# A decoder step in split-precision matmuls: the residual x goes to HBM for the feed-forward stage

## The reference, cut to what matters

```
up = rmsnorm(x, norm_ffn_w) @ w_up            # 1024 -> 2 * 2816
c  = causal_dwconv(up, prefix, conv_w, conv_b)  # width 3, per channel
g, u = c[..., :2816], c[..., 2816:]
x  = x + (silu(g) * u) @ w_down               # 2816 -> 1024
y  = rmsnorm(x, norm_final_w)
```

## Time and profile before

| | |
|---|---|
| median of three runs | 868.1 us |
| span of the profiled execution | 866.2 us |
| what lies around the span (difference to the median) | 1.9 us |
| TensorE busy | 849.0 us (98%) |
| VectorE busy | 553.8 us (64%) |
| ScalarE busy | 364.3 us (42%) |
| GpSimd busy | 76.9 us (9%) |
| granted TensorE clock, mean | 0.996 |

### The profile page before, as it was taken

One profiled execution on the slowest core, in us unless ns is written; L12 is line 12 of the kernel. 1 busy time (PEld: TensorE's weight loads), 2 busy tenths in 40 slices (PEclk: granted clock), 3 DMA queues, 4 the chain that ended last, 5 costly groups with the idle time before them and its releaser, 6 DMA issues.

```text
span 866.2 us, 17354 instructions
## 1 busy us (share of the span) xinstructions
PE 849.0 (98%) x6884; PEld 799.4 (92%) x6884; DVE 553.8 (64%) x981; ACT 364.3 (42%) x652; POOL 76.9 (9%) x149
## 2 busy tenths in 40 slices
PE   6999999999999999999999999999999999999995
PEld 6988878789999999877899999999999999999995
DVE  6444246678574643455355899678697796786754
ACT  6402133366453721344343756244353352443452
POOL 2320000000000000000000321012011110110200
PEclk9999999999999999999999999999999999999998
DMA  9798689721233565579133322223322322231323
GB/s 308 255 369 291 215 325 337 246 93 40 66 99 105 159 248 172 192 270 369 68 110 126 99 65 83 86 77 107 98 86 86 122 75 86 84 102 73 88 78 104
DMA packets 50146, 131.25 MB, mean 152 GB/s; under 512 B 5939, under 2 KB 8503, under 8 KB 49810
## 3 DMA queue, kind: packets, MB, share of 16 engines
q1 hardware_dynamic: 48064, 124.40, 43.5%
q0 software_dynamic: 1712, 5.62, 1.8%
q10 hardware_dynamic: 290, 0.12, 0.1%
HBM read 123.12 MB, written 7.00 MB: 150 GB/s over the span
## 4 chain that ended last, share of the span: by engine, by line
PE 83%; DVE 1%; ACT 0%; issue 0%; DVEq 0%
PE proj L1181 53%; PE proj L1137 3%; PE proj L1198 2%; PE score L1265 2%; PE score L1263 2%; PE score L1264 2%; PE proj L1200 2%; PE proj L1199 2%; PE score L1432 2%; PE T L1265 1%; PE T L1263 1%; PE T L1264 1%; PE score L1398 1%; PE T L1274 1%; PE T L1417 1%; PE score L1467 1%
## 5 line engine op out<-in xcount | busy, mean ns | idle before, releaser
L1181 PE MATMUL proj<-a_hi,w_hi 128*128 128x272 f32 (+1 forms) x740 | 159.7, 290 | 6.4 <-DVE w_lo L1891 6.2
L1532 ACT ACTIVATE w_hi<-w_raw 128x1024 fp32r<-128x1024 f32 (+2 forms) x128 | 118.4, 931 | 109.1 <-PE proj L1181 93.2
L1181 PE MATMUL proj<-a_lo,w_hi 128*128 128x272 f32 (+1 forms) x740 | 158.2, 288 | 0.0
L1181 PE MATMUL proj<-a_hi,w_lo 128*128 128x272 f32 (+1 forms) x740 | 158.0, 288 | 0.0
L1868 DVE TENSOR_TENSOR w_lo<-w_raw,w_hi 128x1024 fp32r<-128x1024 f32 (+2 forms) x128 | 136.3, 1070 | 29.0 <-ACT w_hi L1532 28.8
L1181 PEld LDWEIGHTS proj<-a_hi,w_hi 128*128 128x128 f32 x740 | 118.4, 189 | 13.1 <-issue 6.7
L1181 PEld LDWEIGHTS proj<-a_lo,w_hi 128*128 128x128 f32 x740 | 118.8, 189 | 0.0
L1181 PEld LDWEIGHTS proj<-a_hi,w_lo 128*128 128x128 f32 x740 | 118.4, 189 | 0.0
L1181 PE MATMUL proj<-d_hi,w_hi 128*128 128x272 f32 x448 | 92.5, 287 | 0.0
L1181 PE MATMUL proj<-d_lo,w_hi 128*128 128x272 f32 x448 | 92.1, 287 | 0.0
L1181 PE MATMUL proj<-d_hi,w_lo 128*128 128x272 f32 x448 | 92.1, 288 | 0.0
(11 more groups left out here) (360 smaller groups left out, 1655.7 us busy)
## 6 DMA issues: line engine op xcount, KB each, us to landing
w_raw<-in_w_up SPq DMA_DIRECT2D x28, 512.0 KB, 3.6
w_raw<-in_w_in SPq DMA_DIRECT2D x21, 512.0 KB, 3.8
early_pages<-in_cache_k SPq DMA_DIRECT2D x32, 256.0 KB, 5.8
pages<-in_cache_v SPq DMA_DIRECT2D x32, 256.0 KB, 5.3
c_pages<-in_cache_mem_k SPq DMA_DIRECT2D x16, 512.0 KB, 7.0
c_pages<-in_cache_mem_v SPq DMA_DIRECT2D x16, 512.0 KB, 6.3
p_raw<-in_w_up SPq DMA_DIRECT2D x16, 512.0 KB, 3.9
w_raw<-in_w_down SPq DMA_DIRECT2D x32, 256.0 KB, 2.6
```

What stands on the lines that cost most here:

```text
L1181: mm = pe.matmul(tile_banks(n)[:, half, 0:width], wt, act[:, at, half * HALF:half * HALF + width], start=(k == 0 and a == 0), stop=(k == w ...
L1532: act.activation(w_hi[:, n % W_HI_RING, 0:kt, :], w_raw[:, n % W_RING, 0:kt, :], ACT.Copy).then_inc(w_hi_ready, 1)
```

## The change: what it does

- **x in HBM.** In column 1 SyncE stores x to a new tensor `scratch_x` (step `x_store`, 2.2 MB). The bytes of x in SBUF then hold `p_raw`, `t_raw` and a buffer `down_out`; a second `down_out` lies in `norm_area`. `p_lo` and `t_lo` keep their old places, now apart from the raw data. In column 20, step `x_back` loads x again, in two halves.
- **The 32 adds of columns 4 to 19** are no longer a VectorE addition. ScalarE copies the tile from PSUM to one of the two `down_out` buffers, and GpSimd issues a DMA of it (128 x 544 fp32, 272 KB) that accumulates on `scratch_x`. ScalarE waits before each copy for the accumulating DMA of two tiles earlier. The eight adds of the last group stay on VectorE and wait for the two loads of x.
- **The list of steps of the feed-forward stage is written anew.** TensorE's order of tiles and products is the same. The first pair's weights are loaded in column 4 behind the gate tile's step (before: at the stage's start), since x must be free. Column 4 now makes all three splits of the first pair ahead of its `gate` step. In the later columns, splits, sums and loads of the next pair stand in the paired column, and the last steps of a paired column (`up_in` of the up half, `taps`, `gate`, `act`) stand behind the following gate tile.
- Semaphores are merged: `mix_prefix_loaded` and `fvec_loaded` become one, `rows_loaded` joins `lams_loaded`.

The diff, cut to what the prediction speaks of:

```diff
+    def pair_ends(prev, q):
+        p = PAIRED.index(prev)
+        nearer = [("pair_split", q, 1)], [("pair_hi", q, 2), ("pair_split", q, 2), ("pair_load", q + 1, 1)]
+        ahead, behind = nearer if q < len(PAIRED) else ([], [])
+        return [("pair_out", p, 4)] + ahead + [("up_in", prev, 1)] + behind
+    for i in range(FT):
+        downs = [TILE[step] for step in beside_of(i)]
+        prev_paired = i - 1 in PAIRED
+        if i in PAIRED:
+            q = PAIRED.index(i)
+            more = q + 1 < len(PAIRED)
+            s += [("prod", q, 1), ("prod", q, 2)]
...
+            (hi0, lo0), (hi1, lo1) = (split_next(f) for f in downs)
+            s += [("pair_out", q, 1), ("pair_out", q, 2), ("tile", downs[0])] + hi0
...
+            s += [("prod", q, 5), ("prod", q, 6), ("pair_out", q, 5), ("add", downs[0]), ("pair_out", q, 6)]
+            s += [("sums", q + 1)] * more + [("act", i - 1)] * prev_paired
+            s += [("tile", downs[1])] + hi1 + lo1 + [("pair_hi", q + 1, 0)] * more
+            s += [("prod", q, 7), ("pair_out", q, 7), ("add", downs[1])] + [("pair_split", q + 1, 0)] * more
+            s += [("prod", q, 3)] + [("pair_hi", q + 1, 1)] * more + [("pair_out", q, 3), ("up_in", i, 0), ("prod", q, 4)]
+            s += [("pair_load", q + 2, 0)] * more
             continue
...
+        if prev_paired:
+            s += pair_ends(i - 1, PAIRED.index(i - 1) + 1) + hi0
+            s += [("taps", i - 1, 0)] + lo0 + [("taps", i - 1, 1), ("gate", i - 1), ("up_in", i, 0)] + hi1
+            s += [("act", i - 1)] + lo1 + [("taps", i, 0), ("tile", up_tile), ("up_in", i, 1), ("taps", i, 1), ("gate", i)]
+        elif i + 1 == PAIRED[0]:
+            s += hi0 + hi1 + [("up_in", i, 0)] + lo0 + lo1 + [("pair_load", 0, 0), ("pair_load", 0, 1), ("blend_lo", i - 1), ("taps", i, 0)]
+            s += [("sums", 0), ("tile", up_tile), ("pair_hi", 0, 0), ("pair_hi", 0, 1), ("up_in", i, 1), ("pair_split", 0, 0), ("pair_load", 1, 0)]
+            s += [("pair_hi", 0, 2), ("pair_split", 0, 1), ("taps", i, 1), ("pair_split", 0, 2), ("pair_load", 1, 1), ("gate", i)]
...
+            if i == 1:
+                s.append(("x_store",))
...
+        if i == FT - 2:
+            s.append(("x_back",))
+        for f in downs:
+            hi, lo = split_next(f)
+            s += [("tile", f)] + hi + lo + [("add", f)]
+        s.append(("act", i))
...
+        p_raw = lend(x_area, 0, (2, KT, P))
+        t_raw = lend(x_area, 2 * KT * P, (3, 4, P))
+        down_out = [lend(x_area, 2 * KT * P + 12 * P, (TOK,)), lend(norm_area, 24 * P, (TOK,))]
...
+        def wait_x_free(eng):
+
+            eng.wait_ge(ready["up"], KT)
+            eng.wait_ge(sem("xw_ready"), 8)
+            eng.wait_ge(sem("x_stored"), 16)
...
+                if kind == "x_store":
+                    for n in (KT - 2, KT - 1):
+                        wait_tile_out(sp, TILE["co", "add", n])
+                    sp.dma_start(t["scratch_x"], x[:, :, :]).then_inc(sem("x_stored"), 16)
+                if kind == "x_back":
+                    wait_pair_lo(sp, len(PAIRED) - 1, 2)
+                    for n in range(2):
+                        sp.wait_ge(sem(f"x_added{n}"), 16 * len(X_ADDS[n::2]))
+                    for n in range(2):
+                        sp.dma_start(x[:, 4 * n:4 * n + 4, :], t["scratch_x"][:, 4 * n:4 * n + 4, :]).then_inc(sem(f"x_loaded{n}"), 16)
...
+                if kind == "add" and arg in X_ADDS:
+                    m = X_ADDS.index(arg)
+                    wait_tile_out(pool, arg)
+                    pool.dma_start(t["scratch_x"][:, TILES[arg]["i"], :], down_out[m % 2], accum_op=ALU.add
+                                   ).then_inc(sem(f"x_added{m % 2}"), 16)
...
+                elif kind == "add" and arg in X_ADDS:
+                    m = X_ADDS.index(arg)
+                    act.wait_ge(tile_done, arg + 1)
+                    if m >= 2:
+                        act.wait_ge(sem(f"x_added{m % 2}"), 16 * (m // 2))
+                    else:
+                        wait_x_free(act)
+                    act.activation(halves(down_out[m % 2]), proj[arg % 2][:, :, 0:HALF], ACT.Copy).then_inc(tile_out[arg % 2], 1)
...
-                elif kind == "add":
+                elif kind == "add" and arg not in X_ADDS:
+                    dve.wait_ge(sem(f"x_loaded{TILES[arg]['i'] // 4}"), 32)
```

More of the change, by code:

```diff
@@ L348, in split_next @@
         return [("w_hi", n + 2)] if n + 2 < len(TILES) else [], [("w_lo", n + 2)] if n + 2 < len(TILES) else []
[L350 to L368, removed]
-            continue
[L370 to L390, removed]
-            s.append(("norm", "up"))
[L392 to L404, removed]
@@ new lines, in pair_ends @@
+    def pair_ends(prev, q):
[11 more added lines that the diff above has]
+            if prev_paired:
+                s += pair_ends(i - 1, q)
+            (hi0, lo0), (hi1, lo1) = (split_next(f) for f in downs)
+            s += [("pair_out", q, 1), ("pair_out", q, 2), ("tile", downs[0])] + hi0
+            if prev_paired:
+                s += [("taps", i - 1, 0)] + lo0 + [("taps", i - 1, 1), ("gate", i - 1)]
+            else:
+                s += lo0
+            s += [("prod", q, 5), ("prod", q, 6), ("pair_out", q, 5), ("add", downs[0]), ("pair_out", q, 6)]
[4 more added lines that the diff above has]
+            s += [("pair_load", q + 2, 0)] * more
+            continue
+        gate_tile, up_tile = TILE["up", "gate", i], TILE["up", "up", i]
+        (hi0, lo0), (hi1, lo1) = split_next(gate_tile), split_next(up_tile)
+        s.append(("tile", gate_tile))
+        if i == 0:
+            s.append(("norm", "up"))
+        if prev_paired:
+            s += pair_ends(i - 1, PAIRED.index(i - 1) + 1) + hi0
[5 more added lines that the diff above has]
+            s += [("pair_hi", 0, 2), ("pair_split", 0, 1), ("taps", i, 1), ("pair_split", 0, 2), ("pair_load", 1, 1), ("gate", i)]
+        else:
+            s += hi0 + [("up_in", i, 0)] + lo0
+            if i:
+                s += [("blend_lo", i - 1)] * (i <= 4)
+            if i == 1:
+                s.append(("x_store",))
+            s += [("taps", i, 0), ("tile", up_tile)] + hi1 + [("up_in", i, 1)] + lo1 + [("taps", i, 1), ("gate", i)]
@@ L424 @@
 SCHEDULE = make_schedule()
+X_ADDS = [step[1] for step in SCHEDULE if step[0] == "add" and TILES[step[1]]["phase"] != LAST_DOWN]
 HALVED = {step[1] for step in SCHEDULE if step[0] == "half_tile"}
@@ L982, in _ @@
                 if kind == "pair_load" and arg < len(PAIRED):
[L983 to L987, removed]
+                    j = step[2]
+                    if arg:
+                        wait_pair_lo(sp, arg - 1, j)
+                    else:
+                        wait_x_free(sp)
+                    sp.dma_start(p_raw[:, j, :, :], t["w_up"][((D_FF, 0)[j] + PAIRED[arg] * P) // P, :, :, :]
+                                 ).then_inc(sem(f"slot_landed1_{j}"), 16)
+                if kind == "x_store":
[8 more added lines that the diff above has]
+                        sp.dma_start(x[:, 4 * n:4 * n + 4, :], t["scratch_x"][:, 4 * n:4 * n + 4, :]).then_inc(sem(f"x_loaded{n}"), 16)
                 if kind == "scale":
@@ L2076, in _ @@
                     q, part = step[1:]
[L2077 to L2078 removed]
+                    dve.wait_ge(sem("pair_hi"), 3 * q + part + 1)
+                    if part:
+                        dve.wait_ge(sem("sums_made"), q + 1)
                     if part == 2:
```

33 lines of the change are left out of this document (13 added, 20 removed).

## The result

The changed kernel takes 869.7 us (median of 8 runs, 868.48 to 870.95); the kernel before took 867.44 in the same comparison (8 runs, 866.84 to 869.03). The ratio is 1.0025, 95% interval 1.0015 to 1.0035: slower by about 2.2 us. The profiled execution took 868.48 us with a span of 866.7; it is the fastest of the eight.

The account below looks back on a forecast made before the run. TensorE, busy 849.0 of 866.2 us, was taken to bound the kernel. All terms were 0 except one stop in columns 4 and 5, 0.85 + 0.6 = 1.4 us, added to 868.1: 869.5 us, range 867.4 to 873.0.

Parts of the forecast that it names:

- Adds off VectorE: Columns 4 to 19: 32 adds, 23.0 us, leave VectorE; gain 0, at most 0.24 us, as TensorE waits for nothing.
- Accumulating DMAs: GpSimd's DMAs of down tiles onto x: landing taken as 8 us, bounds 5.5 and 13.8; cost 0.
- the 9.4 us given beside it: Landing of an accumulating DMA estimated from the Trainium skill's figure for GpSimd waiting on the port shared with VectorE.
- the limits of 10.6 and 13.0: Landing times in us above which TensorE's product 7 would wait: 10.6 in the first pair, 13.0 in a steady pair.
- Store and load of x: Store in column 1 (7 us) and reload before the last adds (some 9 us, 20 available): cost 0.
- (a): Column 4: the first pair's load goes out late, so VectorE's sums start 0.5 to 1.5 us late, or 0; 0.6 taken.
- L: Delay of the start of VectorE's sums of the first pair in column 4; 0.6 us taken, range 0 to 1.5.
- (b): Three splits ahead of column 4's gate delay w_lo, so TensorE stops at column 5's first down tile: 0.85 us, bounds 0 to 1.5.
- Sum: Columns 4 and 5: 0.85 + 0.6 = 1.4 us, rounded down; span 867.6, median 869.5 us.
- The stop at the second down tile grows by L: Column 4: TensorE's existing stop of about 0.25 us lengthens by the sums' delay, counted within the 1.4 us.
- Later columns: Even columns behind a pair: VectorE carries 16.7 of 18 us, TensorE's cover is 2.2 us; cost 0.
- Rival D: Faster: VectorE's relief closes hidden TensorE stops, giving at most 867.6 us; head and tail untouched; chance 0.03.

Follow-up runs that it names:

- both edits: Changed kernel with the first pair's load one tile earlier on SyncE and two of its splits back behind the gate: 868.12 us, ratio 1.0007.

## Why the prediction held, and what it missed

- *Adds off VectorE, 0.* Right: 18.7 us less busy time, and no wait of TensorE from 553 to 794.9 us. ScalarE's copy took 0.60 us, under the bound of 0.8.
- *Accumulating DMAs, 0, landing 8.* The cost is right. 7.5 and 7.8 us is what the first pair's two take, while two loads of the next pair and the weights run beside them; the median of all is 4.8. So the value taken was too high for the rest, as was the 9.4 us given beside it, and both stood under the limits of 10.6 and 13.0. ScalarE never waits for one in the changed kernel.
- *Store and load of x, 0.* Right: store 9.3 us, load 6.5 from 807 on, the first add that needs it at 827.08.
- *(a) the late load, L = 0.6.* Right in kind. It was 0.36 in the first profile, 0.15 in the second, and 0.74 to 0.94 in those of the edited kernels that keep it late. The bounds of 0 to 1.5 held all of them; a single value isn't to be had from the rows of before.
- *(b) the splits ahead of the gate, 0.85.* Right in kind, and too small: 1.07 us in every profile of this order in which nothing else waits. The walk along the queues was exact. w_lo ended at 540.7 in before's times, 540.4 without L, which is where the steps put it, and the taps start behind ScalarE's `t_hi`, as worked out. What was off is TensorE's side. The 539.62 of the earlier trace rows is where the chain's previous piece ends; TensorE's own row starts at 539.46, 0.16 earlier. And after a stop the next two matmuls take 0.11 us more.
- *Sum, 1.4.* The stretch grew by 1.43, in part by luck: L came out 0.24 under the value taken and (b) 0.22 over it. That the two simply add is shown: 269.84 + L + 1.07 gives the stretch of six profiles to 0.01 us. "The stop at the second down tile grows by L" held too: `up_in` 0.4.
- *Later columns, 0.* Right: with both edits the stretch is before's to 0.01 us.
- *What was missed.* Rival D's "the head and the tail of the kernel are not touched", and the same assumption in the forecast. No instruction of the tail had changed, but SyncE's list had become longer in total, and a piece of it is fetched at another time: +0.65 us, a third of the whole. It moved the result from 0.16% (1.4 us), "same" by the bound of 0.2%, to 0.25%, "slower", which had a chance of 0.43 against 0.52; the interval of 0.15 to 0.35% leaves the side of the bound open. That the time itself, 869.5 forecast and 869.7 measured, is so close is luck: the kernel before took 867.44 in this comparison, 0.66 us under the 868.1 that I added to, which hides the 0.65 of the tail.

## What to carry to other kernels

Work taken off an engine with slack is worth nothing until it is spent: here moving 32 adds (23 us) off VectorE cost 2.2 us, and the gain came with four more paired columns, for which VectorE then had the room. Where an edit also moves loads or splits, walk the queue at the tightest place instruction by instruction; a sum of durations from the trace before gave the end of the last w_lo to 0.05 us. TensorE's side of a stop is best read from the starts of its matmuls, since the idle time shown (0.80) was 0.27 us short of the cost, and the landing of a load in a burst was known to 0.8 us only. When a tail changes that nobody edited, look at the packets of the instruction queues beside the last output.

## What the runs showed of the hardware

- An accumulating DMA of 128x544 f32 from SBUF to HBM landed in 4.2 to 7.8 us (median 4.8; 8.2 at most in a second profile), a plain one from the same place in 2.3 to 6.8 (3.3); GpSimd's issue took 0.85 against 0.54 us.
- A single 0.01 MB packet of instructions on the DMA engines, in the middle of the output, went with 0.65 us on the last output block (4.3 against 3.6 us to landing, in nine profiles with it and three without); 24 idle instructions on SyncE, hundreds of microseconds earlier, moved it out of the way, 48 on VectorE moved another packet and not this one.
- A burst of three loads (1.31 MB) issued 0.35 us ahead of the same instruction let the sums behind it start over a spread of 0.8 us (L from 0.15 to 0.94) in seven profiles.
- A stop of TensorE shown as 0.80 us idle cost it 1.07 us, from one matmul's start to the next ones'.
